# The start of a one-core layer stack and the order of its recurrence: x split in quarters, six banks for the first tiles, T before U, all masks made ahead

## The chip, the cores and the metric

One core of a Trainium2 chip runs the whole kernel. The metric is the device time of one execution in microseconds, as the median over runs. The engines are TensorE (PE), VectorE (DVE), ScalarE (ACT), GpSimd (POOL) and SyncE (SP), which here only issues transfers. Each has its own instruction stream, in order; they meet through semaphores.

## What is computed

The kernel computes three layers over 256 tokens of 2048 channels. The change touches the start of the first layer and its recurrence. In short form:

```python
h = rms_norm(x, norm_g)
proj = h @ w_in                       # all projections of the first layer
q, k, v, ... = split(proj)            # windowed attention, memory attention
mkv = rms_norm(mem, mem_norm_g) @ x_w_kv
# recurrence, per head, forward and backward in time (12 heads, two directions):
def step(S, inp):
    r_t, d_t, k_t, v_t, kk_t, b_t = inp
    sa = einsum('bhij,bhj->bhi', S, -kk_t)
    S = S * d_t[:, :, None, :] + sa[..., None] * b_t[:, :, None, :] + v_t[..., None] * k_t[:, :, None, :]
    return S, einsum('bhij,bhj->bhi', S, r_t)
```

The normalisation is folded in late: x is multiplied by its gain and goes into the products raw, and each result tile is scaled by one over the root mean square (rstd) when it leaves its bank.

## The kernel before

**Products.** Every weight matrix comes from memory as a stream of 565 tiles (128 output channels by 2048 inputs), each in two units of 8 blocks of 128 by 128, 512 KB. A ring of four units holds them: SP loads `raw`, ACT copies it to `w_hi` (`split_hi`, L284 to L294), DVE writes the rest to `w_lo` (`split_lo`, L296 to L303), and PE does three matmuls of 256 columns for each block (`product`, L310 to L316): high by high, high by low, low by high. The result of a tile gathers in bank 0 or 1 by the tile's parity. A unit's slot is split anew once PE has used it (`units_used`), and loaded anew once its `w_lo` is made (`lo_ready`). `hx` holds x times gain, split in the same way (`act_tile` L381, `dve_tile` L385), 16 blocks.

**Start.** SP issues the first four units. ACT issues `par`, the four quarters of x, the constants, the four quarters of mem and three small tensors (L2687 to L2695), then splits: unit 0, eight blocks of x, unit 1, eight blocks, two more units. DVE follows in the same order, with unit 0 ahead of the x blocks. PE's first tile needs eight blocks of x (`ready`). POOL squares and sums x block by block (L394 to L400), two operations each, then mem in the same way. After tile 1 PE multiplies the sum by ones into bank 2 (`x_norm.pe`, L413), ACT takes the root (L417), DVE the reciprocal (L421), and only then does the first of the 14 tiles of phase `plain` leave its bank (L451). Within the phase ACT's and DVE's streams hold the splitting of mem behind tiles 0 and 1, eight blocks each (L383, L388).

**Recurrence.** `act_rwkv`, `dve_rwkv`, `pool_rwkv` and `pe_rwkv` loop over six pairs of heads. Four weight tiles per pair (`pair_tile`, 64 blocks) run beside it on PE in portions set out by hand: `go(GO_START)` 8 blocks, `go(GO_PREP)` 24, three times `go(GO_GRAM)` 7, the rest one at a time. PE's first matmuls of a pair (`zw`) feed a tanh on ACT (L1055); a chain on DVE (L1102 to L1120) makes decays and keys; then PE forms the products within chunks (`mt`, `kat`, `m`, L1204). Tile 2 of a pair is split on DVE in `dve_pair_tile(v, p, 0)`, behind that chain. The inverse of a 64 by 64 triangle is built in five levels: PE makes X from the masked matrix `ml` and `tm`, ACT copies it (L1082), PE makes U and then T for one direction and then for the other, DVE adds them to `u` (L1160) and `tm` (L1157). POOL makes each level's `ml` (L1043) in one buffer a direction, after PE has used the last.

## Time and profile before

| | us |
|---|---|
| median of 3 runs (lowest, highest) | 3683.31 (3678.11, 3684.11) |
| the profiled execution | 3684.94 |
| its span | 3683.1 |
| PE busy | 3537.9 (96%) |
| DVE busy | 2404.0 (65%) |
| ACT busy | 1627.7 (44%) |
| POOL busy | 366.7 (10%) |

The span runs from the first to the last instruction of the profiled execution; 1.8 us lie around it. Busy PE is summed over its matmuls, whose ends are modelled, so a busy stretch can hide short gaps. The first PE instruction is at 21.25 us. The phase `plain` ends near 126.66 us, the recurrence lies between about 398 and 764 us, six pairs of 61.6 us.

### The profile page before, as it was taken

How to read it: one execution, taken by the hardware profiler on the slowest of the kernel's cores; microseconds unless marked ns; L12 is line 12 of the kernel's file. 1: busy time of each engine (PE TensorE's matmuls, PEld its weight loads, DVE VectorE, ACT ScalarE, POOL GpSimd, SP SyncE). 2: the span in 40 equal slices, each digit the busy share in tenths (PEclk: the TensorE clock that was granted, in tenths of full speed). 3: DMA queues.
4: the chain of work that ended last, by engine and by line, in shares of the span. 5: the costliest groups of instructions: out<-in, count | busy, mean ns of one | idle time of the engine just before them, and what ended most of it. 6: DMA issues, size and time to landing. Idle time of an engine off the chain costs nothing.

```text
span 3683.1 us, 76895 instructions
## 1 busy us (share of the span) xinstructions
PE 3537.9 (96%) x28942; PEld 3295.8 (89%) x28942; DVE 2404.0 (65%) x3377; ACT 1627.7 (44%) x2205; POOL 366.7 (10%) x417
## 2 busy tenths in 40 slices
PE   6999899999999999989999999999999799999997
PEld 6999888889999999989988888889999788888886
DVE  6787666665565467866666666676675665656567
ACT  4456333334444433654444444444344443434344
POOL 6000232310011000221100000010000300000004
PEclk9999999999999999999999999999999999999999
DMA  5544221225565555445565555555544455556564
GB/s 201 164 155 145 87 81 61 81 93 182 182 203 186 183 172 171 149 143 180 180 192 180 190 185 189 181 190 187 182 157 147 142 177 188 194 183 193 182 189 154
DMA packets 165417, 606.14 MB, mean 165 GB/s; under 512 B 18384, under 2 KB 18512, under 8 KB 164992
## 3 DMA queue, kind: packets, MB, share of 16 engines
q1 hardware_dynamic: 163296, 594.62, 50.2%
q10 hardware_dynamic: 1760, 6.80, 0.5%
q8 instruction: 136, 2.23, 0.3%
q0 software_dynamic: 192, 2.23, 0.2%
q14 instruction: 33, 0.27, 0.0%
HBM read 601.47 MB, written 2.10 MB: 164 GB/s over the span
## 4 chain that ended last, share of the span: by engine, by line
PE 86%; DVE 10%; ACT 2%; issue 2%; ACTq 0%; DVEq 0%; POOL 0%
PE bank L329 25%; PE bank L314 14%; PE bank L316 14%; PE bank L315 14%; PE bank L330 13%; PE bank L1204 4%; DVE w_lo L303 3%; ACT w_hi L294 0%; ACT X L2595 0%; DVE mem_hl L388 0%; DVE hx L388 0%; DVE xa L1782 0%; PE bank L1410 0%; DVE tm L1157 0%; DVE nrm_kk L925 0%
## 5 line engine op out<-in xcount | busy, mean ns | idle before, releaser
L294 ACT ACTIVATE w_hi<-raw 128x1024 fp32r<-128x1024 f32 x1130 | 1161.3, 1052 | 905.7 <-PE bank L316 537.8
L303 DVE TENSOR_TENSOR w_lo<-raw,w_hi 128x1024 fp32r<-128x1024 f32 x1130 | 1372.0, 1253 | 103.6 <-ACT w_hi L294 103.4
L329 PE MATMUL bank<-hid,w_hi 128*128 128x512 f32 x2048 | 717.5, 395 | 1.3 <-DVE hid L2025 1.2
L330 PE MATMUL bank<-hid,w_lo 128*128 128x256 f32 x2048 | 572.6, 280 | 0.0
L314 PE MATMUL bank<-hx,w_hi 128*128 128x256 f32 x1568 | 462.7, 295 | 42.4 <-DVE hx L388 23.9
L329 PEld LDWEIGHTS bank<-hid,w_hi 128*128 128x128 f32 x2048 | 384.0, 188 | 93.7 <-issue 2.2
L315 PE MATMUL bank<-hx,w_hi 128*128 128x256 f32 x1568 | 448.3, 286 | 0.0
L316 PE MATMUL bank<-hx,w_lo 128*128 128x256 f32 x1568 | 447.7, 286 | 0.0
L330 PEld LDWEIGHTS bank<-hid,w_lo 128*128 128x128 f32 x2048 | 386.4, 189 | 0.0
L329 PE MATMUL bank<-xh,w_hi 128*128 128x512 f32 x1024 | 358.5, 395 | 19.3 <-issue 17.7
L314 PE MATMUL bank<-u,w_hi 128*128 128x256 f32 (+1 forms) x1280 | 366.8, 287 | 9.5 <-DVE w_lo L303 9.5
L316 PE MATMUL bank<-u,w_lo 128*128 128x256 f32 (+1 forms) x1280 | 367.5, 287 | 0.0
L315 PE MATMUL bank<-u,w_hi 128*128 128x256 f32 (+1 forms) x1280 | 367.1, 287 | 0.0
L329 PE MATMUL bank<-u,w_hi 128*128 128x512 f32 x1024 | 360.6, 397 | 1.0 <-DVE w_lo L303 1.0
L314 PEld LDWEIGHTS bank<-hx,w_hi 128*128 128x128 f32 x1568 | 304.7, 194 | 55.3 <-DVE hx L388 24.2
L315 PEld LDWEIGHTS bank<-hx,w_hi 128*128 128x128 f32 x1568 | 305.1, 195 | 1.0 <-issue 1.0
L316 PEld LDWEIGHTS bank<-hx,w_lo 128*128 128x128 f32 x1568 | 305.1, 195 | 0.0
L330 PE MATMUL bank<-u,w_lo 128*128 128x256 f32 x1024 | 287.3, 281 | 0.0
L330 PE MATMUL bank<-xh,w_lo 128*128 128x256 f32 x1024 | 286.8, 280 | 0.0
L314 PEld LDWEIGHTS bank<-u,w_hi 128*128 128x128 f32 x1280 | 244.0, 191 | 10.9 <-DVE w_lo L303 10.7
L329 PEld LDWEIGHTS bank<-xh,w_hi 128*128 128x128 f32 x1024 | 192.6, 188 | 64.4 <-issue 18.1
L315 PEld LDWEIGHTS bank<-u,w_hi 128*128 128x128 f32 x1280 | 244.8, 191 | 0.0
(453 smaller groups left out, 6393.4 us busy)
## 6 DMA issues: line engine op xcount, KB each, us to landing
raw<-stream SPq DMA_DIRECT2D x1130, 512.0 KB, 4.1
x_raw<-xT ACTq DMA_DIRECT2D x4, 512.0 KB, 10.4
mem_raw<-memT ACTq DMA_DIRECT2D x4, 512.0 KB, 18.0
x_res<-xT POOLq DMA_DIRECT2D x1, 2048.0 KB, 8.4
out<-X SPq DMA_DIRECT2D x4, 512.0 KB, 2.6
cst<-consts ACTq DMA_DIRECT2D x1, 1504.0 KB, 15.0
w_sb<-w ACTq DMA_DIRECT2D x1, 384.0 KB, 19.5
a_sb<-a ACTq DMA_DIRECT2D x1, 384.0 KB, 19.9
```

The lines of the kernel that those rows point to most:

```text
L294: nc.scalar.activation(w_hi[:, slot], raw[:, slot], ACT.Copy).then_inc(hi_ready, 1)
L303: nc.vector.tensor_tensor(w_lo[:, slot], raw[:, slot], w_hi[:, slot].bitcast(F), ALU.subtract).then_inc(lo_ready, 1)
L314: nc.tensor.matmul(dst, w_hi[:, slot, j], hi, start=first, stop=False)
L315: nc.tensor.matmul(dst, w_hi[:, slot, j], lo, start=False, stop=False)
L316: return nc.tensor.matmul(dst, w_lo[:, slot, j], hi, start=False, stop=last)
L329: nc.tensor.matmul(bank[:], w_hi[:, slot, j], both, start=kt == 0, stop=False)
L330: last = nc.tensor.matmul(bank[:, T:], w_lo[:, slot, j], hi, start=False, stop=kt == KT - 1)
L1204: last = nc.tensor.matmul(out[h], lhs[h], rhs[h], start=start, stop=stop)
```

## The change

The four quarters of x and the constants move from ACT's queue to SP's, in the order x quarter 0, unit 0, the other quarters, units 1 to 3, constants. ACT issues only `par` at first, runs a one-element activation, and splits x a quarter at a time; DVE splits four blocks before unit 0's low part, the other twelve behind it. PE's first tile waits for x by quarters. ACT squares x after its splits, POOL sums the squares, and mem is issued after the squares, the small tensors later still. Phase `plain` is written out tile by tile: tiles 2 to 5 go to banks 4 to 7, weights are split four tiles ahead of the first scaling, and the statistic is taken after tile 3. Mem is split two blocks a tile from tile 4 on. In the recurrence PE makes T before U, five buffers a direction hold the masks and POOL makes them in a row, the first unit of tile 2 is split at the head of the pair's loop on ACT and DVE, and PE starts a pair's first tile when the last pair's tile 2 (not 3) has left its bank. The lists of step names follow.

```diff
+PLAIN_BANKS, PLAIN_AHEAD = 6, 4
 CENTRED = {7: (0, 1), 8: (2, 3), 9: (4, 5), 10: (6, 7), 11: (8, 9), 12: (10, 11), 13: (12, 13), 14: (14,)}
...
-            def pe(self, pe):
-                pe.wait_ge(self.sums, 2 * KT + 1)
+            def act_square(self, act, kt, squares, squared):
+                nc.scalar.activation(squares[:, kt], self.src[:, kt], ACT.Square).then_inc(squared, 1)
+            def pool_squares(self, pool, squares, squared):
+                self.pool_start(pool)
+                pool.wait_ge(self.lo, KT)
+                for kt in range(KT):
+                    pool.wait_ge(squared, kt + 1)
+                    pool.wait_ge(self.sums, kt + 1)
+                    nc.gpsimd.tensor_tensor(self.acc[:], self.acc[:], squares[:, kt], ALU.add).then_inc(self.sums, 1)
+            def pe(self, pe, count=2 * KT + 1):
+                pe.wait_ge(self.sums, count)
                 nc.tensor.matmul(banks[2][:, 0:self.n], const("ones"), self.acc[:], start=True, stop=True).then_inc(self.stat, 1)
...
+        x_squares = at("x_squares", Z, [P, KT, T])
+        x_squared = sem("x_squared")
+        warm, warm_set = at("warm", Z + 20 * K, [P, 1]), sem("warm_set")
         mem_out, plain_out = (sem(n) for n in ("mem_out", "plain_out"))
+        def plain_bank(t):
+            return banks[2 + t] if 2 <= t < PLAIN_BANKS else banks[t % 2]
+        def dve_plain(v, late):
+            for t in range(COUNT["plain"]):
+                tile = Tile(FIRST["plain"], t)
+                if t == 0:
+                    for k in range(PLAIN_AHEAD):
+                        split_lo(v, Tile(FIRST["plain"], k).later())
+                    x_norm.dve_rstd(v)
+                tile_done(v, tile)
+                nc.vector.tensor_tensor(pl[:, t], plain_bank(t)[:, 0:T], x_norm.rstd[:], ALU.mult).then_inc(plain_out, 1)
+                if t >= PLAIN_AHEAD:
+                    split_lo(v, tile.later())
+                hooked(tile, late)
+        def act_plain(act, hooks):
+            for t in range(COUNT["plain"]):
+                tile = Tile(FIRST["plain"], t)
+                if t == 0:
+                    for k in range(PLAIN_AHEAD):
+                        split_hi(act, Tile(FIRST["plain"], k).later())
+                if t >= PLAIN_AHEAD:
+                    split_hi(act, tile.later())
+                hooked(tile, hooks)
+        def pe_plain(pe, after):
+            for t in range(COUNT["plain"]):
+                tile = Tile(FIRST["plain"], t)
+                if t in (PLAIN_BANKS, PLAIN_BANKS + 1):
+                    pe.wait_ge(plain_out, t - PLAIN_BANKS + 1)
+                elif t >= PLAIN_BANKS + 2:
+                    pe.wait_ge(plain_out, t - 1)
+                for q in range(4):
+                    if t == 0:
+                        pe.wait_ge(x_norm.lo, 4 * q + 4)
+                    pe.wait_ge(lo_ready, tile.units(q // 2 + 1))
+                    for kt in range(4 * q, 4 * q + 4):
+                        last = product(plain_bank(t)[:, 0:T], hx, (2 * tile.parity + q // 2) % RING, kt % HALF, kt, kt == 0, kt == KT - 1)
+                    if q % 2 == 1:
+                        last.then_inc(units_used, 1)
+                hooked(tile, after)
...
-            for k, n in enumerate(("abd", "rbd", "bbd", "kbd", "mt", "tm", "brt", "btok", "ktok", "nkatv", "kat", "krt", "u", "x", "ml")):
+            for k, n in enumerate(("abd", "rbd", "bbd", "kbd", "mt", "tm", "brt", "btok", "ktok", "nkatv", "kat", "krt", "u", "x")):
                 w[n] = at(f"{n}{d}", o + K * k, [P, NCH, CH])
+            w["ml"] = {l: at(f"ml{l}_{d}", o + 13 * K + K * l, [P, NCH, CH]) for l in range(1, LEVELS)}
             for k, n in enumerate(("e1", "e2", "e3", "th")):
...
-                        + [f"{n}{l}_{d}" for d in D2 for n in (("U", "T") if l < LEVELS - 1 else ("U",))]]
+                        + [f"{n}{l}_{d}" for d in D2 for n in (("T", "U") if l < LEVELS - 1 else ("U",))]]
                      + [f"{n}{s}_{d}" for s in ST for n in ("W", "SA", "S", "Y") for d in D2
...
-                        pe.wait_ge(gate_kept, p * BESIDE + max(k // KT - 1, 0))
+                        if p > 0 or k >= 2 * KT:
+                            pe.wait_ge(gate_kept, p * BESIDE + k // KT - 1)
                     if kt % HALF == 0:
...
                         for d, w in enumerate(dirs):
-                            need(pool, rw_p, f"X{l - 1}_{d}", p)
-                            rw_o.done(nc.gpsimd.tensor_tensor(w["ml"][:], w["mt"][:], level(l), ALU.mult), f"ml{l}_{d}")
+                            if l == 2 and d == 0:
+                                need(pool, rw_v, "q", p)
+                            rw_o.done(nc.gpsimd.tensor_tensor(w["ml"][l][:], w["mt"][:], level(l), ALU.mult), f"ml{l}_{d}")
                 need(pool, rw_p, f"X{LEVELS - 1}_1", p)
...
             with act.Fori(0, PAIRS) as p:
+                split_hi(act, pair_tile(p, 0).later(), (0,))
...
                     rw_a.done(nc.scalar.activation(w["e3"][:], w["s"][:], ACT.Exp, scale=HALF_DECAY), f"e3{d}")
-                split_hi(act, pair_tile(p, 0).later())
+                split_hi(act, pair_tile(p, 0).later(), (1,))
                 split_hi(act, pair_tile(p, 1).later())
...
-                            need(act, rw_p, f"T{l - 1}_{d}", p)
+                            need(act, rw_p, f"U{l - 1}_{d}", p)
                         rw_a.done(nc.scalar.activation(w["x"][:], value_part(bank_of(d, 1), 0), ACT.Copy), f"X{l}_{d}")
...
             with v.Fori(0, PAIRS) as p:
+                split_lo(v, pair_tile(p, 0).later(), (0,))
...
                 rw_v.done(nc.vector.tensor_tensor(rkv[:, p], rkv[:, p], ks[:], ALU.mult), "q")
-                dve_pair_tile(v, p, 0)
+                dve_pair_gate(v, p, 0)
+                split_lo(v, pair_tile(p, 0).later(), (1,))
...
                             rw_v.done(nc.vector.tensor_tensor(w["tm"][:], w["tm"][:], value_part(bank_of(d, 0), 0), ALU.add), f"T{l}_{d}")
-                        else:
-                            need(v, rw_p, f"U{l}_{d}", p)
+                        need(v, rw_p, f"U{l}_{d}", p)
                         rw_v.done(nc.vector.tensor_tensor(w["u"][:], w["u"][:], value_part(bank_of(d, 2), 0), ALU.add), f"U{l}_{d}")
...
                             need(pe, rw_v, f"T{l - 1}_{d}", p)
-                        rw_p.done(each(bank_of(d, 1), w["ml"], w["tm"]), f"X{l}_{d}")
+                        rw_p.done(each(bank_of(d, 1), w["ml"][l], w["tm"]), f"X{l}_{d}")
...
                             need(pe, rw_v, f"U{l - 1}_{d}", p)
-                        rw_p.done(each(bank_of(d, 2), w["x"], w["u"]), f"U{l}_{d}")
                         if l < LEVELS - 1:
                             rw_p.done(each(bank_of(d, 0), w["u"], w["x"]), f"T{l}_{d}")
+                        rw_p.done(each(bank_of(d, 2), w["x"], w["u"]), f"U{l}_{d}")
                 for s in ST:
...
         def _(sp):
-            for k in range(RING):
+            def x_in(q):
+                sp.dma_start(x_raw[:, 4 * q:4 * q + 4], xT[:, 4 * q:4 * q + 4]).then_inc(in_x[q], 16)
+            def raw_first(k):
                 sp.dma_start(raw[:, k], stream[k]).then_inc(raw_in[k], 16)
+            x_in(0)
+            raw_first(0)
+            for q in range(1, 4):
+                x_in(q)
+            for k in range(1, RING):
+                raw_first(k)
+            sp.dma_start(cst[:], consts).then_inc(in_cst, 16)
             rounds = N_UNITS // RING
...
         def _(pool):
-            for norm, parts in ((x_norm, in_x), (mem_norm, in_mem)):
-                norm.pool_start(pool)
-                for q in range(4):
-                    pool.wait_ge(parts[q], 16)
-                    for j in range(4):
-                        norm.pool_tile(pool, 4 * q + j)
+            x_norm.pool_squares(pool, x_squares, x_squared)
+            mem_norm.pool_start(pool)
+            for q in range(4):
+                pool.wait_ge(in_mem[q], 16)
+                for j in range(4):
+                    mem_norm.pool_tile(pool, 4 * q + j)
             pool_rwkv(pool)
...
             act.dma_start(par[:], params).then_inc(in_par, 16)
-            for q in range(4):
-                act.dma_start(x_raw[:, 4 * q:4 * q + 4], xT[:, 4 * q:4 * q + 4]).then_inc(in_x[q], 16)
-            act.dma_start(cst[:], consts).then_inc(in_cst, 16)
+            act.wait_ge(warm_set, 1)
+            nc.scalar.activation(warm[:], warm[:], ACT.Identity)
+            act.wait_ge(in_par, 16)
+            def split_x(q):
+                act.wait_ge(in_x[q], 16)
+                for kt in range(4 * q, 4 * q + 4):
+                    x_norm.act_tile(act, kt)
+            split_x(0)
+            split_hi(act, Tile(0, 0), (0,))
+            for q in range(1, 4):
+                split_x(q)
+            split_hi(act, Tile(0, 0), (1,))
+            split_hi(act, Tile(0, 1))
+            for kt in range(KT):
+                x_norm.act_square(act, kt, x_squares, x_squared)
             for q in range(4):
                 act.dma_start(mem_raw[:, 4 * q:4 * q + 4], memT[:, 4 * q:4 * q + 4]).then_inc(in_mem[q], 16)
-            act.dma_start(w2_sb[:], w2).then_inc(in_lora, 16)
-            act.dma_start(a2_sb[:], a2).then_inc(in_lora, 16)
-            act.dma_start(wgu_sb[:], wgu).then_inc(in_lora, 16)
-            def split_all(norm, parts, half=(0, 1)):
-                for kt in range(HALF * half[0], HALF * (half[-1] + 1)):
-                    if kt % 4 == 0:
-                        act.wait_ge(parts[kt // 4], 16)
-                    norm.act_tile(act, kt)
-            split_hi(act, Tile(0, 0), (0,))
-            act.wait_ge(in_par, 16)
-            split_all(x_norm, in_x, (0,))
-            split_hi(act, Tile(0, 0), (1,))
-            split_all(x_norm, in_x, (1,))
-            split_hi(act, Tile(0, 1))
             def after_plain0():
                 x_norm.act_root(act)
                 act_lam(act)
-                split_all(mem_norm, in_mem, (0,))
-            act_split_phase(act, "plain", {0: after_plain0, 1: lambda: split_all(mem_norm, in_mem, (1,)), 8: lambda: act_squares(act, 0),
-                                           10: lambda: act_roots(act, range(4)), 12: lambda: act_squares(act, 1)}, peel=COUNT["plain"] // 2)
+                act.dma_start(w2_sb[:], w2).then_inc(in_lora, 16)
+                act.dma_start(a2_sb[:], a2).then_inc(in_lora, 16)
+                act.dma_start(wgu_sb[:], wgu).then_inc(in_lora, 16)
+            def split_mem(kt):
+                if kt % 4 == 0:
+                    act.wait_ge(in_mem[kt // 4], 16)
+                mem_norm.act_tile(act, kt)
+                mem_norm.act_tile(act, kt + 1)
+            def with_mem(t, f):
+                return (lambda: (split_mem(2 * (t - 4)), f())) if t in range(4, 12) else f
+            own = {8: lambda: act_squares(act, 0), 10: lambda: act_roots(act, range(4)), 12: lambda: act_squares(act, 1)}
+            act_plain(act, {0: after_plain0, **{t: with_mem(t, own.get(t, lambda: None)) for t in range(4, 13)}})
...
         def _(v):
-            def split_all(norm, half=(0, 1)):
-                for kt in range(HALF * half[0], HALF * (half[-1] + 1)):
-                    norm.dve_tile(v, kt, kt + 1)
+            nc.vector.memset(warm[:], 0.0).then_inc(warm_set, 1)
+            v.wait_ge(in_par, 16)
+            for kt in range(4):
+                x_norm.dve_tile(v, kt, kt + 1)
             split_lo(v, Tile(0, 0), (0,))
-            v.wait_ge(in_par, 16)
-            split_all(x_norm, (0,))
+            for kt in range(4, KT):
+                x_norm.dve_tile(v, kt, kt + 1)
             split_lo(v, Tile(0, 0), (1,))
-            split_all(x_norm, (1,))
             split_lo(v, Tile(0, 1))
-            dve_scaled_phase(v, "plain", x_norm, pl, plain_out, {0: lambda: x_norm.dve_rstd(v)},
-                             {0: lambda: split_all(mem_norm, (0,)), 1: lambda: split_all(mem_norm, (1,)),
-                              **{11 + b: lambda b=b: dve_factors(v, [b]) for b in range(3)}}, peel=COUNT["plain"] // 2)
+            def split_mem(kt):
+                for k in (kt, kt + 1):
+                    mem_norm.dve_tile(v, k, k + 1)
+            late = {t: lambda t=t: split_mem(2 * (t - 4)) for t in range(4, 11)}
+            late[11] = lambda: (split_mem(14), dve_factors(v, [0]))
+            late[12], late[13] = lambda: dve_factors(v, [1]), lambda: dve_factors(v, [2])
+            dve_plain(v, late)
             dve_scaled_phase(v, "mem_kv", mem_norm, mkv, mem_out, {0: lambda: mem_norm.dve_rstd(v)}, {0: lambda: dve_factors(v, [3]), 1: lambda: dve_factors(v, [4]), 2: lambda: dve_factors(v, [5]),
...
                 pe.wait_ge(in_cst, 16)
-                x_norm.pe(pe)
-            plain_phase(pe, "plain", hx, plain_out, before=lambda k: x_norm.ready(pe, k), after={1: x_stat, 9: lambda: pe_stats(pe, range(4)), 13: lambda: pe_stats(pe, (4, 5))}, peel=COUNT["plain"] // 2)
+                x_norm.pe(pe, KT + 1)
+            pe_plain(pe, {3: x_stat, 9: lambda: pe_stats(pe, range(4)), 13: lambda: pe_stats(pe, (4, 5))})
```

## Rows read from the trace of the kernel before

**Rows 1.** Windows: busy us (and count) by engine, clock, DMA share, GB/s.
```profile
0.00:21.25 21.25, 0.00 (x0) 0.00 (x0) 8.07 (x10) 10.44 (x20) 11.96 (x21) 1.00 0.92 354
21.25:71.20 49.95, 38.56 (x242) 37.55 (x243) 39.13 (x40) 19.98 (x32) 43.72 (x50) 0.86 0.44 148
71.20:126.66 55.46, 55.46 (x443) 53.55 (x442) 30.35 (x29) 25.09 (x25) 0.00 (x0) 1.00 0.54 173
```

**Rows 2.** Timeline, PE, first 70 us: start, length, instruction [idle before <-releaser].
```profile
21.25 0.58 PE L314 MATMUL bank<-hx,w_hi 128*128 128x256 f32 x1 [21.25 <-DVE hx L388]
...
44.39 0.55 PE L314 MATMUL bank<-hx,w_hi 128*128 128x256 f32 x1 [4.16 <-DVE w_lo L303]
```

**Rows 3.** Windows (columns as rows 1): PE before and after the clock rises.
```profile
44.40:47.70 3.30, 3.30 (x15) 3.30 (x16) 3.30 (x4) 3.30 (x7) 3.06 (x4) 0.50 0.62 179
47.70:51.70 4.00, 4.00 (x35) 3.96 (x33) 4.00 (x6) 3.83 (x9) 3.54 (x6) 0.99 0.31 119
```

**Rows 4.** DMA issues: KB each, median us from issue to landing.
```profile
par<-params ACTq DMA_DIRECT2D x1, 241.0 KB, 4.1
```

**Rows 5.** Timeline, ACT: the start of the kernel.
```profile
3.88 2.23 ACTq L2692 DMA_DIRECT2D mem_raw<-memT  x4
...
10.80 1.28 ACT L294 ACT_TABLE_LOAD   x1 [10.80 <-issue]
12.09 1.06 ACT L294 ACTIVATE w_hi<-raw 128x1024 fp32r<-128x1024 f32 x1
13.06 3.29 ACT L383 ACTIVATE hx<-x_raw,par 128x256 fp32r<-128x256 f32 x8
```

**Rows 6.** Timeline, ACT: two neighbouring 256-column operations in a head pair.
```profile
649.13 0.40 ACT L1065 ACTIVATE e<-sx 128x256 f32<-128x256 f32 x1
649.44 0.40 ACT L1066 ACTIVATE e<-s 128x256 f32<-128x256 f32 x1
```

**Rows 7.** Timeline, DVE: splits, with POOL at work (first two) and without.
```profile
14.65 6.54 DVE L388 SCALAR_TENSOR_TENSOR hx<-x_raw,par,hx 128x256 fp32r<-128x256 f32 x8
...
42.81 2.98 DVE L303 TENSOR_TENSOR w_lo<-raw,w_hi 128x1024 fp32r<-128x1024 f32 x2
...
71.75 2.35 DVE L303 TENSOR_TENSOR w_lo<-raw,w_hi 128x1024 fp32r<-128x1024 f32 x2
...
397.78 2.45 DVE L931 SCALAR_TENSOR_TENSOR kkn<-rkv,par,nrm_kk 128x256 f32<-128x256 f32 x6
```

**Rows 8.** Groups, first 70 us: busy us, mean ns | idle before.
```profile
L400 POOL TENSOR_TENSOR x_norm_acc<-x_norm_acc,x_norm_sq 128x256 f32<-128x256 f32 x16 | 13.8, 865 | 1.3
```

**Rows 9.** Timeline, PE: one head pair of the recurrence (636 to 664 us).
```profile
641.63 0.38 PE L314 MATMUL bank<-hx,w_hi 128*128 128x256 f32 x1 [0.63 <-DVE rkv L971]
...
656.08 0.68 PE L1204 MATMUL bank<-abd,bbd 64*64 64x64 f32 x16 [0.81 <-DVE e_end L1120]
...
660.00 0.36 PE L314 MATMUL bank<-hx,w_hi 128*128 128x256 f32 x1 [0.90 <-DVE w_lo L303]
```

**Rows 10.** Timeline, ACT and DVE: the start of the same pair.
```profile
645.49 1.28 ACT L1055 ACT_TABLE_LOAD   x1 [3.39 <-PE bank L1226]
646.78 0.47 ACT L1055 ACTIVATE th<-bank,hw_sb 128x256 f32<-128x256 f32 x1
...
647.29 0.29 DVE L1102 TENSOR_SCALAR th<-th 128x256 f32<-128x256 f32 x1 [3.44 <-ACT th L1055]
```

**Rows 11.** Timeline, PE: the same place of the first head pair.
```profile
411.07 0.68 PE L1204 MATMUL bank<-abd,bbd 64*64 64x64 f32 x16 [2.45 <-DVE e_end L1120]
```

**Rows 12.** Timeline, PE: first matmuls (X) of levels 1, 2, 4 and 5.
```profile
673.98 1.15 PE L1204 MATMUL bank<-tm,ml 64*64 64x64 f32 x32
...
677.06 1.13 PE L1204 MATMUL bank<-tm,ml 64*64 64x64 f32 x21
...
683.35 1.48 PE L1204 MATMUL bank<-tm,ml 64*64 64x64 f32 x32
...
686.50 1.48 PE L1204 MATMUL bank<-tm,ml 64*64 64x64 f32 x32
```

2 lines of the change are left out of this document (1 added, 1 removed).

## The prediction

> **What bounds the kernel now.** I read the windows first, cut at the places where PE's work changes, then PE's timeline at the start, then the streams of DVE and ACT, and last one head pair. Between 71.20 and 126.66 us PE has no idle time at all, and ahead of that it has plenty [rows 1]: nothing for 21.25 us, then 38.56 us of busy time in 49.95 us, at a mean clock of 0.86. So the end moves one for one with the moment at which PE's stream is unbroken. A tile's length at full speed is in the same row: nine tiles of 48 matmuls and some 3.5 us of statistics fill 55.46 us, which is 5.77 a tile, 0.12 a matmul; I use 5.76.
>
> Five tiles end by 71.20. Five times 5.76 and 0.45 for the statistic's matmul are 29.25 us; PE took 71.20. The other 41.95 us are 21.25 of start, 11.39 idle (49.95 less 38.56) [rows 1] and 9.3 of slow clock. The idle parts end on DVE: the start on a split of x, a later one of 4.16 us on `w_lo` [rows 2]. Behind most of these gaps PE runs at half clock, 1.2 GHz, for some 3.3 us (clock 0.50, 15 matmuls in 3.30 us) before it is back at 2.4 GHz (35 in 4.00) [rows 3]. DVE is the late one because it is slow and has too much in front. Eight blocks of x take it 6.54 us, 0.82 each, while POOL works; an operation of the same kind and shape without POOL takes 0.41 (six in 2.45). Two weight units take 2.98 with POOL and 2.35 without [rows 7]. And the first scaling waits for POOL's sum, a root and a reciprocal, with eight blocks of mem behind it.
>
> **The start, worked out.** ACT is now the longest chain. `par` is issued at 0.75 us and takes 4.1 us [rows 4]; it leads its queue before and after, so ACT starts at 4.85, its table load (1.28 us, now ending at 12.09) being done under that wait [rows 5]. Then: sixteen x blocks at 3.29 / 8 = 0.41, 6.6 us; four weight units at 1.0 (1.06 long, with some overlap), 4.0 us [rows 5]; sixteen squares. Before has no square of this shape; two neighbouring operations of it without a per-partition scale stand 0.31 apart [rows 6], with one 0.41 [rows 5], so 5.0 to 6.6 us, and I take 5.0, since a square has no such scale. Four issues of mem take 2.2 us [rows 5]. That puts ACT at 22.7; I add 0.3 for quarters of x that arrive just in time (`par`, unit 0 and four quarters are 2.9 MB, wanted at 10.9; at the 354 GB/s of the start [rows 1], with 2 us of silence taken off, 3.2 MB have come by then). First unit of tile 2: 1.06 on ACT and 1.2 on DVE (2.35 / 2) [rows 7], so 25.3 us.
>
> PE can begin tile 0 after four blocks of x and unit 0: ACT has these at 7.6, DVE's low part at 8.9. Its first two quarters run at half clock till 14.1. DVE, without POOL at 0.41 a block, is done with x at 12.9 right behind ACT, with unit 1 at 14.8, with tile 1's units at 16.2 and 17.4. So tile 0 ends near 17.8 and tile 1 near 23.5. PE then waits 1.8 us for tile 2. Gaps of that size are followed by the slow stretch in some places and not in others (the 2.45 us at 411.07 [rows 11] is followed by matmuls at full spacing, the 4.16 us is not [rows 2]); half of its 1.6 us, 0.8, goes into the sum. Tiles 2, 3, 4 and the statistic are 17.28 + 0.45. Tile 4 ends at 25.3 + 0.8 + 17.7 = 43.8 us; before it was 71.2. **Gain 27.4 us.**
>
> What hides the rest. POOL's sum: sixteen additions at 0.865 [rows 8] from 15.9, done at 29.8, wanted after tile 3 at 37.6. Root, reciprocal and four scalings end by 43, and tile 6, the first that needs a bank back, starts at 49.6; without the six banks it would be late. ACT has a root, two small operations with table loads and three issues before tile 6's split: free by 46, wanted 1 us of copy and 1.2 us of DVE ahead of 49.6. Per tile DVE then has a scaling (0.4), two units (2.4 to 3.0) and two mem blocks (1.6 with POOL), 5.0 of the 5.76 us. The last two mem blocks share tile 11 with a reciprocal, which makes DVE 1.3 us late there; PE needs that split four units later, so nothing.
>
> The bounds of this part: squares at 0.41 and no luck with the clock take 2.4 off; a first unit that lands and is split without any wait, with tile 2 following tile 1 at once, adds 2.6. So 25 to 30 for what rows price, and 21 if DVE's speed does not change (below).
>
> **The recurrence.** Three edits. (a) **T before U.** In a level PE does X, X, then four groups of 0.47 us. Level 1, whose second X waits for nothing, lasts 677.06 - 673.98 = 3.08 us; level 4 lasts 686.50 - 683.35 = 3.15, the second X waiting for DVE's late T [rows 12]. With T first that wait goes, and what is next is ACT's copy of X, which already sets level 1. So 0.07 for each of levels 2 to 5: 0.3 a pair, 1.7 us in six. (b) **The gate.** PE's start of a pair waits 0.63 us for tile 3's scaling [rows 9]; tile 2's was long ago: 0.6 in each of five pairs. (c) **Unit 0 of tile 2 early.** It removes 0.90 us of waiting for `w_lo` [rows 9] and puts something in front of the tanh. ACT's copy can only start when PE has used the slot, which is when PE starts `zw`; the table load goes with the first activation of the loop, so load and copy end 1.28 + 1.0 us after that, and DVE's 1.2 us split follows before the chain at L1102. Before, load and tanh took 645.49 to 647.25 [rows 10]. From PE's own start: DVE's chain begins 647.29 before; after, with PE 0.6 earlier, at 644.3 + 2.35 + 1.2 = 647.87. The idle time before `mt` grows from 0.81 [rows 9] to about 2.0, the 0.90 goes, and PE meets its next block at 659.5 where it was 660.00 [rows 9]. DVE's masks of `mt` come as much earlier, since one unit fewer lies ahead of them. So (b) and (c) together are 0.5 in each of five pairs, 2.5 us. The first pair has no gate to save and its ACT starts late, so there load, copy and split all lie on the chain: 1.76 later at 411.07 [rows 11], less 0.90, so 0.9 lost. Masks ahead: eight POOL operations of 0.7 to 0.9 follow the last of level 1's, in a stretch where DVE reads banks and not SBUF twice; no PE wait ends on POOL here before, so nothing gained or lost. **Gain 1.7 + 2.5 - 0.9 = 3.3 us**; between a loss of 0.5 (the chain pays 1.76 in every pair: 10.6 against 5.4, 3.0 and 1.7) and, by the third rival below, a gain of 10.
>
> **Sum.** 27.4 + 3.3 = 30.7 us. The profiled execution would be 3684.94 - 30.7 = 3654.2; it lies 1.6 above the median of the runs. Against the median: 3683.31 - 30.7 = 3652.6 us. About 0.2% (7 us) is what a measurement tells from no change.
>
> **Rivals.**
> DVE keeps 0.82 us a block (12%). That length is seen only with POOL at work [rows 7], and no row read here has this line without it. Then x is done at 19.9 instead of 12.9, unit 1 at 21.1, tile 2 starts near 31.4: gain 21 + 3, time 3659. For it: the line writes rounded values and takes a scale per partition, which L931 does only in part. Against it: the ratio of two to L931, with the same shape.
> The Trainium skill, page SBUF, State Buffer, section on who interferes with whom, says that a DVE operation with two SBUF inputs and a POOL operation that reads SBUF block each other for the whole instruction. By that rule the block falls to 0.41 once POOL is silent, which is the forecast; the trace has 0.82 and 0.41 in the two conditions but for different lines, so it agrees without proving it.
>
> The pair's head costs more than it saves (13%). If the load comes in front of the copy and a second one in front of the tanh, the chain has 1.28 us more in each of six pairs: 3.3 - 7.7 = 4.4 lost, time 3660. For it: six table loads now, one in each pair, so the loop forgets its set. Against: copies in the loop run after the tanh's set without a load.
>
> The table load is done before the slot's wait ends (12%). Then the chain begins 1.28 us earlier in each pair and PE's idle time at `mt` is back to 0.8: 7 us more, time 3646. For it nothing but order; the load at 645.49 waited for PE [rows 10].
>
> Slower than before (2%): POOL's sum is handed over square by square, and the scalings of all tiles hang on it. Tile 6 needs its bank at 49.6, and root, reciprocal and first scaling take 4 us. With 0.865 us a step the sum is there at 29.8 [rows 8]. From (45.6 - 15.9) / 16 = 1.9 us a step PE begins to stand, and from 1.9 + 30.7 / 16 = 3.8 us the kernel is slower than before. The slowest condition now, two operations a block under contention, is twice 0.865, 1.73. A time of 3690 needs 4.2.
>
> The change does little at the start because something unseen paces it, the arrival of x above all (3%): 3672.
>
> **Chances and range.** Forecast 58%, 3652.6. Range 3644 to 3662: it takes in the start between 21 and 30 and the recurrence between a loss of 4 (second rival) and a gain of 10, not all at their worst together. Faster by over 0.2%: 0.96; within 0.2%: 0.02; slower: 0.02.
>
> **What would show it.** First matmul near 9 us; DVE's x blocks 0.41 apart; tile 4's scaling at 44, phase `plain` over at 99 instead of 126.66. In a pair: no `w_lo` wait, no gate wait, about 2 us ending on `e_end`, levels of 3.08. What would make it wrong: x blocks at 0.82, a first matmul after 12, a second table load in a pair, or any wait in the later tiles of `plain` on rstd.

## The result and the profile after

The changed kernel takes 3645.99 us (median of 5 runs, 3641.99 to 3655.65) against 3684.11 of five runs of the kernel before taken beside it: 38.1 us less. The ratio estimated from the runs is 0.9888, 95% interval 0.9875 to 0.9902; the quotient of the two medians, 0.9897, lies inside that interval. Applied to the 3683.31 of the runs shown above, the ratio gives 3642, some 2 us under the lower end of the range (3644); the difference of 38.1 gives 3645, just inside it. The forecast was 3652.6, a gain of 30.7. The direction and the start were right; the recurrence gave some 11 us where I had 3.3. The third rival had 3646, nearer than the forecast.

The windows of after; the first two together cover the work of all three in [rows 1], the third the attention (columns as there: busy us and count by engine, clock, DMA share, GB/s):

```profile
0.00:44.20 44.20, 31.76 (x244) 31.39 (x245) 26.63 (x34) 29.38 (x52) 25.13 (x30) 1.00 0.90 342
44.20:99.40 55.20, 55.20 (x441) 53.28 (x440) 42.30 (x45) 31.24 (x41) 26.32 (x25) 1.00 0.53 166
99.40:370.00 270.60, 262.89 (x2077) 248.29 (x2075) 218.04 (x346) 146.10 (x215) 2.26 (x3) 1.00 0.48 150
```

Tile 4 is done at 44.2 instead of 71.2, nine tiles then take 55.2 without idle time as before, and `plain` ends at 99.4 instead of 126.66. The start, PE's idle times with what ended them:

```profile
9.93 0.55 PE L317 MATMUL bank<-hx,w_hi 128*128 128x256 f32 x1 [9.93 <-DVE w_lo L306]
...
15.82 0.36 PE L317 MATMUL bank<-hx,w_hi 128*128 128x256 f32 x1 [0.95 <-DVE w_lo L306]
```
```profile
37.75 0.67 PE L429 MATMUL bank<-x_norm_acc,cst 128*128 128x256 f32 x2 [1.55 <-POOL x_norm_acc L424]
```

and DVE in the same stretch:

```profile
6.50 1.67 DVE L391 SCALAR_TENSOR_TENSOR hx<-x_raw,par,hx 128x256 fp32r<-128x256 f32 x4 [5.62 <-ACT hx L386]
...
9.71 4.83 DVE L391 SCALAR_TENSOR_TENSOR hx<-x_raw,par,hx 128x256 fp32r<-128x256 f32 x12
...
44.21 0.42 DVE L476 TENSOR_TENSOR pl<-bank,x_norm_rstd 128x256 f32<-128x256 f32 x1 [1.93 <-PE bank L319]
```

The four blocks of x take 1.67 us and the next twelve 4.83, 0.40 each, against 6.54 for eight [rows 7]. The first matmul is at 9.93, one gap of 0.95 follows, and the only other one is new: 1.55 at 37.75 for POOL's sum, whose additions take 0.73 to 1.81 us each (ns least/median/most, then first and last start):

```profile
L424 POOL TENSOR_TENSOR x_norm_acc<-x_norm_acc,x_squares x16: 732/1132/1810, 16.7 to 36.1; 128x256 f32<-128x256 f32 x16
```

In the recurrence the waits of PE (line, who ended them: us, times, longest) were, in [rows 9], 0.63 for the gate, 0.81 on `e_end` and 0.90 for `w_lo`, in each pair. After:

```profile
PE bank L1274 <- DVE e_end L1190: 6.8, 6, 4.1
...
PE bank L1274 <- DVE u L1230: 0.4, 1, 0.4
```

The gate and `w_lo` are gone. `e_end` holds the first pair for 4.13 us and the other five for 0.53. ACT at the head of a pair shows why it isn't 2.0 as I had it:

```profile
606.82 1.06 ACT L297 ACTIVATE w_hi<-raw 128x1024 fp32r<-128x1024 f32 x1 [0.40 <-PE bank L319]
607.90 1.28 ACT L297 ACT_TABLE_LOAD   x1
609.70 1.06 ACT L297 ACTIVATE w_hi<-raw 128x1024 fp32r<-128x1024 f32 x1 [0.51 <-PE bank L319]
610.66 0.46 ACT L1124 ACTIVATE th<-bank,hw_sb 128x256 f32<-128x256 f32 x1
```

The first line is still the last pair's. The table load, 1.28 us, runs at 607.90, ahead of the wait for the slot that PE gives back, and is over 0.51 us before PE ends that wait at 609.70. The copy of unit 0 then starts at once and the tanh follows it.

**Where to measure.** The last phases scatter more than the change's parts are worth. From the first `ybd` (DVE, right behind the recurrence) to the end sixteen profiles, all with the same code there, take 2900.4 to 2917.4 us. A time of the whole kernel from one execution therefore says little about a change of 1 to 3 us. So single profiles are compared by three marks ahead of that: the last matmul on `pr` (end of the attention), PE's first matmul behind `e_end` in each pair, and the first `ybd`. Of before and after the first `ybd`:

```profile
L1377 DVE TENSOR_TENSOR ybd<-kkn,grs x2: 1751/1753/1755, 773.4 to 775.2; 64x1536 f32<-64x1536 f32 x2
```
```profile
L1447 DVE TENSOR_TENSOR ybd<-kkn,grs x2: 1751/1753/1755, 734.5 to 736.3; 64x1536 f32<-64x1536 f32 x2
```

773.4 and 734.5: 38.9 us, close to the 38.1 of the medians; the spans, 3683.1 and 3646.9, have 36.2, since after happened to be 2.7 slower behind the mark (2912.4 against 2909.7).

### The profile page after: what moved, and what is told of

It reads as the page before. It is cut to its first block, busy times and chain, and to the rows that moved or that the text cites. A ratio compares the mean times of both kernels' runs of the same rounds, so it can differ in the third digit from the quotient of the medians.

```text
span 3646.9 us, 76911 instructions
## 1 busy us (share of the span) xinstructions
PE 3532.4 (97%) x28942; PEld 3288.7 (90%) x28942; DVE 2394.9 (66%) x3378; ACT 1633.6 (45%) x2222; POOL 352.0 (10%) x401
## 3 DMA queue, kind: packets, MB, share of 16 engines
q10 hardware_dynamic: 1040, 3.16, 0.2%
## 4 chain that ended last, share of the span: by engine, by line
PE 86%; DVE 9%; ACT 3%; issue 2%; POOL 1%; DMA 0%; DVEq 0%; ACTq 0%; POOLq 0%
PE bank L332 26%; PE bank L317 14%; PE bank L318 13%; PE bank L319 13%; PE bank L333 13%; PE bank L1274 5%; DVE w_lo L306 2%; ACT w_hi L297 1%; POOL x_norm_acc L424 1%; DVE xa L1852 0%; ACT X L2665 0%; PE bank L1480 0%; DVE nrm_kk L990 0%; ACT x L1151 0%; DVE xa L1845 0%
```

## The experiments

All marks in us ("step" is the distance of two pairs' first matmul behind `e_end`, in the steady pairs; "recurrence" is last `pr` to first `ybd`, "rest" first `ybd` to the end of the span):

| kernel | last `pr` | first pair | step | first `ybd` | recurrence | rest |
|---|---|---|---|---|---|---|
| before | 387.0 | 411.07 | 60.99 | 773.4 | 386.4 | 2909.7 |
| after | 359.7 | 385.54 | 58.40 | 734.5 | 374.8 | 2912.4 |
| after_again | 359.9 | 387.15 | 58.40 | 736.1 | 376.2 | 2912.6 |
| start_only | 359.7 | 385.34 | 60.98 | 746.8 | 387.1 | 2902.2 |
| rec_only | 388.4 | 415.20 | 58.40 | 763.4 | 375.0 | 2906.2 |
| unit_late | 359.9 | 385.49 | 59.63 | 739.7 | 379.8 | 2914.8 |
| gate_back | 359.9 | 385.67 | 59.28 | 738.5 | 378.6 | 2914.0 |
| u_first | 359.8 | 385.60 | 58.90 | 737.0 | 377.2 | 2904.9 |
| masks_back | 359.8 | 385.59 | 58.40 | 734.3 | 374.5 | 2911.2 |
| late_load | 359.8 | 387.13 | 61.37 | 750.6 | 390.8 | 2913.6 |
| pool_squares | 367.2 | 393.04 | 58.40 | 742.0 | 374.8 | 2910.4 |
| two_banks | 375.0 | 400.79 | 58.40 | 749.0 | 374.0 | 2912.4 |
| x_on_act | 362.1 | 387.95 | 58.40 | 737.6 | 375.5 | 2912.0 |
| stat4 | 358.4 | 385.47 | 58.40 | 734.3 | 375.9 | 2900.4 |
| first_late | 359.7 | 383.54 | 58.40 | 731.4 | 371.7 | 2917.4 |
| both | 358.0 | 380.41 | 58.40 | 728.3 | 370.3 | 2911.6 |

A step of after's loop repeats within 0.02 us behind the first one, and the last `pr` of kernels with after's start within 0.2; rec_only, whose start is that of before, has it 1.4 later. The first step is longer by what the first pair's slow clock costs (59.95 in after). Seven profiles have some 5 us at a granted clock of 0.66 to 0.73 from the last `pr` on, which lengthens the column "recurrence" (by 1.4 in after_again against after): start_only, rec_only, after_again, unit_late, late_load, stat4 and first_late; the other nine have 1.00 there. Every row is one profile; unit_late, gate_back, u_first, masks_back, pool_squares, two_banks, x_on_act and first_late ran once and have no median.

**The two halves and the scatter.** start_only takes the transfers, quarters, squares on ACT and six banks; rec_only takes T ahead of U, unit 0, the gate and the masks; after_again is after itself.

> The start of after (order of transfers, quarters of x, squares of x on ACT, six banks) with the recurrence of before. By the two profiles the start is worth 27.2 us (scaling of tile 4 at 44.21 against 71.41), so the span should be 27 shorter than before and 9 longer than after, the median near 3656. If the missing part of the gain (the medians differ by 38.1, the two profiled executions by 36.2, my sum says 30.7) lay in the start, something behind tile 4 would be shorter too, and this kernel would gain 30 or more. In the recurrence a pair should be back at 61.56 us with 0.90 of waiting for w_lo and 0.6 for the gate.

> The start of before with the recurrence of after (T ahead of U, unit 0 of tile 2 ahead of the chain, no wait for tile 3's gate, masks ahead). Theory: the table load runs before the slot's wait ends, each pair is 2.48 us shorter (59.08), and the whole gain is 9 us, so a median near 3675 and a ratio near 0.9975. The forecast on record would have it at 3.3 us (3680, ratio 0.9991). If start and recurrence are independent, the gains of this kernel and of the start alone add up to that of after.

> After, unchanged, to see how much of 38.1 against 36.2 us is the scatter of runs. Theory: the profile's 36 us are the change's worth and the medians of few runs move by 2 to 4 us; the ratio then lies between 0.988 and 0.991, the span within 1 us of 3646.9. Rival: the change has a further effect of 4 us that one profile does not show; then the ratio is again 0.9888 or lower and the difference of the spans is 40.

Measured: start_only 3662.17 us (3650.78 to 3671.01, 5 runs), ratio 0.9940 (0.9925 to 0.9954); rec_only 3673.83 (11 runs), 0.9964 (0.9953 to 0.9976); after_again 3646.64 (4 runs), 0.9889 (0.9875 to 0.9904), beside 3686.37 of before. By the marks the first `ybd` comes 26.6 earlier with the start alone, 10.0 with the recurrence alone, 38.9 and 37.3 with both. The sum of the parts, 36.6, is 2.3 and 0.7 short of that; 1.4 of it is what rec_only is late at its last `pr`, ahead of anything that it changes. So start and recurrence are independent as far as this scatter lets one see. By the marks start_only is where it was expected (26.6 for 27), while its median is 6 us above the 3656 expected; the part behind the marks scatters by more than that. after_again's span, 3648.7, was expected within 1 us of 3646.9; rec_only was expected at 3675, with a gain of 9. The second profile of after has the 1.6 in one place, half clock for a few matmuls behind the attention's last wait. The same stretch in after, then in after_again (columns as rows 1, clock third from the end):

```profile
359.60:364.60 5.00, 5.00 (x44) 5.00 (x43) 2.39 (x3) 2.91 (x4) 0.00 (x0) 1.00 0.44 142
```
```profile
359.60:364.60 5.00, 5.00 (x31) 5.00 (x32) 2.51 (x3) 1.86 (x4) 0.00 (x0) 0.66 0.44 146
```

Like with like, the recurrence is 11.6 us shorter (before's 386.4 to after's 374.8, both at full clock there) or 10.9 (start_only's 387.1 to after_again's 376.2, both with that stretch).

**The parts of the recurrence, each undone alone.**

unit_late, in ACT's loop (in DVE's the same):

```diff
-                split_hi(act, pair_tile(p, 0).later(), (0,))
...
-                split_hi(act, pair_tile(p, 0).later(), (1,))
+                split_hi(act, pair_tile(p, 0).later())
```

gate_back, in PE's tiles beside the pairs:

```diff
-                        if p > 0 or k >= 2 * KT:
-                            pe.wait_ge(gate_kept, p * BESIDE + k // KT - 1)
+                        pe.wait_ge(gate_kept, p * BESIDE + max(k // KT - 1, 0))
```

u_first (PE's matmuls and the waits of ACT and DVE to match), and masks_back, where `ml` is one buffer for each direction:

```diff
-                        + [f"{n}{l}_{d}" for d in D2 for n in (("T", "U") if l < LEVELS - 1 else ("U",))]]
+                        + [f"{n}{l}_{d}" for d in D2 for n in (("U", "T") if l < LEVELS - 1 else ("U",))]]
```

```diff
+                            need(pool, rw_p, f"X{l - 1}_{d}", p)
+                            rw_o.done(nc.gpsimd.tensor_tensor(w["ml"][:], w["mt"][:], level(l), ALU.mult), f"ml{l}_{d}")
```

> After with unit 0 of tile 2 copied and split behind the chain again, as before. Theory: the load goes to the tanh and waits for PE again, w_lo's 0.90 us of waiting is back, and the idle time ahead of mt goes from 0.53 to 0.8: a pair of 60.3 us instead of 59.08, the five intervals 300.5. Rival: the unit's place is worth nothing as such and the gain is gate, T and masks; then a pair stays under 59.5.

> After with PE waiting for tile 3's gate at the start of a pair again. Theory: 0.6 us of waiting in each of five pairs, and the chain starts that much later: a pair of 59.7, the five intervals 297.6. Rival: the head's other waits move up, DVE scales tile 3 in time, and the wait costs 0 to 0.2.

> After with U ahead of T in each level, as before. Theory: levels 2 to 5 wait for DVE's late T again, 0.07 each, and a wait of 0.4 for u stands in each pair: 59.4 to 59.8 a pair instead of 59.08, the five intervals 296.1 to 298. The forecast had 0.3 a pair for it. Rival: with the masks made ahead T is in time either way, and a pair stays at 59.1.

> After with one mask buffer in each direction, so that POOL makes each level's mask behind the X of the level before. The forecast had the masks at nothing, since no PE wait ends on POOL in before. Theory: a pair within 0.2 us of 59.08. Rival: the masks carry the part of the 2.48 us a pair that w_lo (0.90), the gate (0.63), T (0.3) and the idle time ahead of mt (0.3) leave, 0.3 a pair; then 59.4.

Measured: steps of 59.63, 59.28, 58.90 and 58.40 against 58.40, so unit 0 is worth 1.23 us a pair, the gate 0.88, T ahead of U 0.50 and the masks nothing. The sum, 2.61, is the whole difference of before and after (60.99 - 58.40 = 2.59). The expectations start from a pair of 59.08. That is the distance from the first start of `abd` (383.6) to the last (679.0) over five, which takes in the 1.8 us between the two directions of one pair and the first pair's 1.55 of half clock; the steady step is 58.40, and their absolute figures are too high by that. What they wanted on top (1.2, 0.6, 0.3 to 0.7, 0) is what came, but for the gate, which gave 0.88. PE's waits in unit_late, then one pair's gate in gate_back:

```profile
PE bank L1271 <- DVE e_end L1188: 6.5, 6, 2.5
PE bank L317 <- DVE w_lo L306: 5.4, 6, 0.9
```
```profile
609.27 0.28 PE L319 MATMUL bank<-hx,w_lo 128*128 128x256 f32 x1
610.18 0.39 PE L317 MATMUL bank<-hx,w_hi 128*128 128x256 f32 x1 [0.62 <-DVE rkv L1036]
610.40 0.28 PE L318 MATMUL bank<-hx,w_hi 128*128 128x256 f32 x1
```

0.90 for `w_lo` is back, and `e_end` is at 0.81 instead of 0.53: 1.18 of the 1.23. In gate_back the wait of 0.62 is seen. The other 0.26 of its 0.88 lie at the two ends of the gap, as the rows show: a matmul of this stream is given as 0.28 long but the next one starts 0.12 behind it when nothing waits, so a break costs 0.16 more than the idle time says, and the first matmul behind it holds the next one for 0.22 instead of 0.12. Of T ahead of U I had 0.07 in each of four levels. The X groups of levels 2 and 3 in u_first (with the wait behind the last level) and in after:

```profile
642.68 1.46 PE L1275 MATMUL bank<-tm,ml 64*64 64x64 f32 x32
...
645.82 1.48 PE L1275 MATMUL bank<-tm,ml 64*64 64x64 f32 x32
...
655.37 0.33 PE L1275 MATMUL bank<-nkatv,u 64*64 64x64 f32 x4 [0.41 <-DVE u L1231]
```
```profile
640.74 1.10 PE L1274 MATMUL bank<-tm,ml 64*64 64x64 f32 x32
...
643.85 1.10 PE L1274 MATMUL bank<-tm,ml 64*64 64x64 f32 x32
```

Levels of 3.14, 3.15 and 3.16 against three of 3.11 are 0.12 a pair; 0.41 is the wait for `u` behind the last level, which stood in five of the six pairs before and now stands only in the last. I had not counted it. (Together 0.53, for a measured 0.50.)

**The place of the table load.** late_load adds the slot's wait once more, ahead of everything in the pair:

```diff
             with act.Fori(0, PAIRS) as p:
+                act.wait_ge(units_used, pair_tile(p, 0).later().units(1 - RING))
                 split_hi(act, pair_tile(p, 0).later(), (0,))
```

> After with one more wait of ACT at the head of each pair, for the slot's last use, placed ahead of the table load, so that the load runs behind that wait as my forecast had it. Theory (the load hides behind the slot's wait): load, copy and DVE's split come 1.28 us later, PE's idle time on e_end grows from 0.53 to about 1.8 us, a pair from 59.08 to 60.4, the five intervals between the first and the last mt from 294.6 to 301, and the mark behind the recurrence (first ybd) from 735 to 741 to 743. Rival (the place of the load doesn't matter and my 3.3 us were wrong elsewhere): a pair stays at 59.1.

Measured: 3666.05 us (3657.09 to 3667.34, 4 runs), ratio 0.9942 (0.9923 to 0.9961); a step of 61.37, 2.97 more than after and even 0.4 more than before. The recurrence takes 390.8, longer than that of before. ACT and PE in one pair:

```profile
617.20 1.06 ACT L297 ACTIVATE w_hi<-raw 128x1024 fp32r<-128x1024 f32 x1 [0.40 <-PE bank L319]
620.20 1.28 ACT L297 ACT_TABLE_LOAD   x1 [1.94 <-PE bank L319]
621.49 1.06 ACT L297 ACTIVATE w_hi<-raw 128x1024 fp32r<-128x1024 f32 x1
622.46 0.46 ACT L1125 ACTIVATE th<-bank,hw_sb 128x256 f32<-128x256 f32 x1
```
```profile
632.49 0.97 PE L1275 MATMUL bank<-abd,bbd 64*64 64x64 f32 x16 [1.95 <-DVE e_end L1191]
633.24 1.07 PE L1275 MATMUL bank<-abd,kbd 64*64 64x64 f32 x16
634.10 1.07 PE L1275 MATMUL bank<-bbd,abd 64*64 64x64 f32 x16
```

The load now stands behind the slot's wait, as I had it in the forecast, and `e_end` costs 1.95 (I had 2.0). What neither the forecast nor the expectation (60.4 a pair, first `ybd` at 741 to 743) had is what follows: the groups of 16 matmuls stand 0.75 and 0.86 apart, where before has 0.51 and 0.47 behind the wait of 2.45 in [rows 11]. Before's next two groups, then the clock of that stretch in late_load and of the same one in after:

```profile
411.58 0.63 PE L1204 MATMUL bank<-abd,kbd 64*64 64x64 f32 x16
412.05 0.63 PE L1204 MATMUL bank<-bbd,abd 64*64 64x64 f32 x16
```
```profile
632.40:636.40 4.00, 3.91 (x80) 3.91 (x82) 3.58 (x10) 0.00 (x0) 0.02 (x1) 0.57 0.00 0
```
```profile
620.60:624.60 4.00, 3.90 (x104) 3.83 (x105) 3.58 (x10) 0.66 (x1) 0.02 (x1) 1.00 0.01 4
```

0.57 is a mix of the two levels, 2.4 and 1.2 GHz. From the first to the last of the six groups late_load takes 3.93 us and after 2.38, 1.55 more; with 1.42 of idle time that is the 2.97. (The 1.42 is 0.14 more than the load's 1.28; that rest is open.) So the place of the load is worth 3 us in each pair, more than the 2.59 of all the edits together.

**The start, one piece undone at a time.**

The edits of pool_squares (POOL squares x again, and ACT doesn't), two_banks, x_on_act (SP issues the weight units alone) and stat4:

```diff
-            x_norm.pool_squares(pool, x_squares, x_squared)
+            for norm, parts in ((x_norm, in_x), (mem_norm, in_mem)):
+                norm.pool_start(pool)
...
+                        norm.pool_tile(pool, 4 * q + j)
```

```diff
-PLAIN_BANKS, PLAIN_AHEAD = 6, 4
+PLAIN_BANKS, PLAIN_AHEAD = 2, 2
-            pe_plain(pe, {3: x_stat, 9: lambda: pe_stats(pe, range(4)), 13: lambda: pe_stats(pe, (4, 5))})
+            pe_plain(pe, {1: x_stat, 9: lambda: pe_stats(pe, range(4)), 13: lambda: pe_stats(pe, (4, 5))})
```

```diff
+            for q in range(4):
+                act.dma_start(x_raw[:, 4 * q:4 * q + 4], xT[:, 4 * q:4 * q + 4]).then_inc(in_x[q], 16)
+            act.dma_start(cst[:], consts).then_inc(in_cst, 16)
```

```diff
-            pe_plain(pe, {3: x_stat, 9: lambda: pe_stats(pe, range(4)), 13: lambda: pe_stats(pe, (4, 5))})
+            pe_plain(pe, {4: x_stat, 9: lambda: pe_stats(pe, range(4)), 13: lambda: pe_stats(pe, (4, 5))})
```

> After with POOL squaring and summing x as it arrives, as before, and no squares on ACT. Tests the term that carried the start: DVE's sixteen x blocks at 0.40 us without POOL. Theory: they go back to 0.82 (6.5 us more in all), tile 1 and tile 2 wait for DVE, and tile 4's scaling comes 3 to 6 us later than 44.2, although ACT has 5 us less to do and POOL's sum is there earlier. Rival (the block's length was set by what the line computes): they stay at 0.40, and with ACT free earlier tile 4 ends sooner than 44.2.

> After with two banks for the first tiles instead of six and the matmul of x's sum behind tile 1. Theory: PE stands behind tile 1 until POOL's sum is there (37.6), then for root, reciprocal and scaling (some 4 us), so tile 2 starts near 42 instead of 24: 15 to 20 us later, and PE behind it runs at half clock for 3 us. Rival: POOL adds faster while PE and DVE stand (0.87 instead of 1.30 a step), which gives 7 us of it back: 8 to 13.

> After with the quarters of x and the constants issued on ACT's queue behind par and the weight units alone on SP's. The forecast had the order of transfers at no cost of its own (x just in time, 0.3 us). Theory: ACT issues five more transfers (0.55 each) ahead of its table load, all under the wait for par, so the start moves by less than 1 us; what decides is the arrival of x and unit 0, which now share the engines sooner: first matmul 9.5 to 11.5, tile 4's scaling 43.5 to 46. Rival: arrival paces the start, the later x quarters wait behind four weight units, and tile 4 comes 3 us or more later.

> After with the matmul of x's sum behind tile 4 instead of tile 3. Theory: the 1.55 us that PE waits for POOL's additions at 37.75 us go (the sum is there at 37.6, tile 4 ends at about 42), while root, reciprocal and first scalings come some 4 us later and still precede tile 6's need of a bank at 49: 1.5 us less than after. Rival: the later scalings make PE wait for a bank at tile 6, 0.5 to 3 us, and the kernel is no faster than after.

pool_squares has its last `pr` 7.5 us later than after, and tile 4's scaling as much; 3 to 6 were expected. DVE and PE:

```profile
6.64 3.30 DVE L391 SCALAR_TENSOR_TENSOR hx<-x_raw,par,hx 128x256 fp32r<-128x256 f32 x4 [5.76 <-ACT hx L386]
...
11.53 9.82 DVE L391 SCALAR_TENSOR_TENSOR hx<-x_raw,par,hx 128x256 fp32r<-128x256 f32 x12
```
```profile
11.75 0.55 PE L317 MATMUL bank<-hx,w_hi 128*128 128x256 f32 x1 [11.75 <-DVE w_lo L306]
...
14.91 0.58 PE L317 MATMUL bank<-hx,w_hi 128*128 128x256 f32 x1 [0.26 <-DVE hx L391]
...
23.04 0.55 PE L317 MATMUL bank<-hx,w_hi 128*128 128x256 f32 x1 [5.30 <-DVE w_lo L306]
```

The same line in the same kernel, 0.82 us a block with POOL at work and 0.40 without: the rival that DVE keeps 0.82 is out. The rule of the Trainium skill (page SBUF, State Buffer, who interferes with whom), which the forecast could only set beside two different lines, is now borne out on one line as to the contention. That each engine stands still for the whole of the other's operation is not: while DVE stands idle a POOL operation of this shape takes 0.61 or 0.73 us (`mem_norm_sq` and `mem_norm_acc` in after, at 43.08 and 43.78), so with DVE's 0.40 strictly in turn a block would take 1.0 to 1.1 us, and 0.82 was measured. In PE's stream tile 2 waits 5.30 for its split. two_banks undoes three things at once (the banks, the place of the statistic, and weights split four tiles ahead) and costs 15.3 at `pr`; PE's gaps:

```profile
35.32 1.19 PE L429 MATMUL bank<-x_norm_acc,cst 128*128 128x256 f32 x2 [10.48 <-POOL x_norm_acc L424]
39.23 0.58 PE L317 MATMUL bank<-hx,w_hi 128*128 128x256 f32 x1 [2.72 <-DVE pl L476]
```

POOL's sum came at 35.3 instead of 37.75, so the rival's faster additions (18.4 us for sixteen instead of 20.9) gave back 2.4 us and not 7; the theory's 15 to 20 holds. Six banks with the sum behind tile 3 are the largest piece of the start. x_on_act costs 2.4: its first x block on ACT waits for `x_raw` till 8.50 instead of for `par` till 5.88, and PE begins at 12.55. The five issues take ACT's queue 2.6 us, all under a wait; what counted is that x landed later when its transfers were issued beside the weights' and not ahead of them. Tile 4's scaling came at 46.64, between the theory's 46 and the rival's 3 us. stat4 takes the new 1.55 us away: last `pr` 1.3 earlier, 3642.06 us (4 runs), ratio 0.9886 (0.9870 to 0.9902). At the first `ybd` only 0.2 to 1.8 us are left of it, since this profile has the slow stretch behind `pr` (clock 0.68), and the medians can't tell it from after.

**The first pair.** first_late writes the first pair out ahead of the loop, on ACT and DVE, and leaves unit 0 behind the chain there; `both` adds the edit of stat4.

```diff
-            with act.Fori(0, PAIRS) as p:
-                split_hi(act, pair_tile(p, 0).later(), (0,))
+            def one(p, head=False):
+                if not head:
+                    split_hi(act, pair_tile(p, 0).later(), (0,))
...
-                split_hi(act, pair_tile(p, 0).later(), (1,))
+                split_hi(act, pair_tile(p, 0).later(), (0, 1) if head else (1,))
...
+            one(0, True)
+            with act.Fori(1, PAIRS) as p:
+                one(p)
```

> After with the first pair written out ahead of the loop on ACT and DVE, and in it unit 0 behind the chain as before; pairs 2 to 6 as in after. Theory: the first wait on e_end falls from 4.13 to 2.45 us and the half clock behind it goes, while 0.90 of waiting for w_lo comes back: from the last weight of the attention (start of the last pr matmul) to the first ybd 2.3 us less than the 374.8 to 376.2 of after, and later pairs stay at 58.40. Rival: the long wait comes from ACT's lateness after the attention, whatever stands first; then e_end stays near 4. A second rival: code written out costs its own fetches, and the pair gains nothing.

> The first pair as in first_late, and the matmul of x's sum behind tile 4 as in stat4. Theory: 2.3 + 1.5 us less than after, a mark (first ybd) of 731 to 732.5 where after has 734.5 and 736.1, and a median of 3641 to 3643 against 3646 of after. Rival: the scatter of the later phases (2900 to 2913 us behind that mark in the profiles so far) covers it, and the medians do not tell it from after.

In after the first pair pays 4.13 us and half clock behind it; in the kernel `both` it pays 0.72 and 0.59:

```profile
385.54 0.68 PE L1274 MATMUL bank<-abd,bbd 64*64 64x64 f32 x16 [4.13 <-DVE e_end L1190]
386.06 0.97 PE L1274 MATMUL bank<-abd,kbd 64*64 64x64 f32 x16
386.82 1.06 PE L1274 MATMUL bank<-bbd,abd 64*64 64x64 f32 x16
```
```profile
380.41 0.68 PE L1282 MATMUL bank<-abd,bbd 64*64 64x64 f32 x16 [0.72 <-DVE e_end L1195]
...
384.01 0.36 PE L317 MATMUL bank<-hx,w_hi 128*128 128x256 f32 x1 [0.59 <-DVE w_lo L306]
```

The recurrence is 371.7 us in first_late (with the slow stretch behind `pr`; 376.2 in after_again) and 370.3 in `both` (without; 374.8 in after): 4.5 less, twice what I expected, since the wait on `e_end` fell not to 2.45 but to 0.7. ACT in first_late shows the rest:

```profile
374.49 0.48 ACT L1125 ACTIVATE th<-bank,hw_sb 128x256 f32<-128x256 f32 x1 [6.13 <-DVE kkn L996]
...
376.35 1.28 ACT L1134 ACT_TABLE_LOAD   x1
377.65 0.42 ACT L1134 ACTIVATE e<-s 128x256 f32<-128x256 f32 x1
```

Written out, the first tanh needs no table load, and the load stands ahead of the exponentials, where ACT in after waits 0.94 us for DVE anyway (at 378.31). In after's first pair the load stands behind ACT's wait for DVE's `kkn` (at 373.28, with 6.36 idle ahead of it), so there load and copy both delay the tanh. The kernel `both` takes 3642.05 us (3633.55 to 3648.00, 5 runs), ratio 0.9872 (0.9856 to 0.9889). Its first `ybd` is at 728.3, earlier than the 731 to 732.5 expected; after has 734.5 and 736.1. It is the best kernel of the study by that mark; its interval overlaps that of after, as its rival said.

## Why the prediction missed

**The start: right.** 27.2 by tile 4's scaling (44.21 against 71.41), 27.3 at the last `pr`, 26.6 at the first `ybd` with the start alone; forecast 27.4. Its terms were less good than its sum. First matmul at 9.93 instead of 8.9, since `par` was waited for till 5.88, 1.0 longer (its transfer took 5.1, not 4.1). The issues of mem, 2.2 us in my sum, cost ACT nothing: their rows (17.56 to 18.89) lie beside squares 0.31 apart, and tile 2's first copy ran at 21.11 instead of 23.0. That removed the gap of 1.8 before tile 2 with its 0.8 of slow clock. POOL's sixteen additions took 1.30 each instead of 0.865, ended at 37.6 instead of 29.8, and PE waited 1.55. Two late terms and one early one cancelled, so that the sum came within 0.2 us is luck in part; squares at 0.31 and x blocks at 0.40 were as worked out.

**T ahead of U: right mechanism, too small.** 0.50 a pair instead of 0.3. The forecast's own term, DVE's late T, gave only 0.12; the other 0.41 is the wait for `u` that it had left out.

**The gate: right mechanism, a little small.** 0.88 a pair instead of 0.6: the idle time was read rightly, and the 0.26 at its two ends were left out.

**Unit 0 ahead of the chain: the step that failed.** I wrote that "ACT's copy can only start when PE has used the slot [...] the table load goes with the first activation of the loop, so load and copy end 1.28 + 1.0 us after that". The copy does wait; the load does not. It runs while ACT waits, the chain starts 1.28 us earlier, and with the gate (b) and (c) are 2.11 a pair and not 0.5. That is the third rival. It had 7 us for five pairs at 12%, for which I saw "nothing but order"; late_load is the direct test: it adds one wait, for something that the copy waits for anyway, and so moves the load behind it, and it measures 2.97 a pair. The rows tell the two cases apart by where the idle time stands: in [rows 10] and in late_load the load itself is what PE releases (1.94 in late_load) and the activation follows without a pause; in after the load has no idle time ahead of it and the activation has 0.51. A wait in front of the load holds both, a wait between them holds the activation alone. I had read [rows 10] as if it held for every place. The source doesn't tell which of the two it will be: before's tanh and after's copy both have their `wait_ge` on the line above the activation, yet the load ran behind the first and ahead of the second. What decides it, no run here shows.

**A second error hid in the same step**: I took 1.2 us more of idle time in each pair at its face value. late_load shows that it would have brought half clock and 1.55 us on top. Had the load stood where I put it, (b) and (c) would have lost 2.97 - 2.11 = 0.86 us a pair instead of gaining 0.5, and the recurrence would have been 3.7 longer than before (390.8 against 387.1 in start_only, both with the slow stretch behind `pr`). That is nearly the size of the second rival, 4.4 lost, by another mechanism. The one question of where the load stands decided between the two ends.

**The first pair**: forecast 0.9 lost; 1.68 more on `e_end` as worked out (1.76), less the 0.90, but 1.55 of half clock behind a wait of 4.13. [rows 11] had shown none behind 2.45.

The sum by sections: last `pr` to `e_end` of the first pair 1.8 lost, five steps 12.4 gained, the last pair 0.9: some 11.6. With 27.3 that is 38.9.

## What to carry over

Before pricing an engine's table load, find in a trace on which side of the wait it stands: with the idle time on the load's own row, or on the row of the activation behind it. In the second case the load cost nothing here, since the wait was longer than it, and the copy at the loop's head became a place for the load to hide. For a place that no trace shows yet, give both cases a chance and a price. Price idle time on PE twice, as idle and as what the clock does behind it: here 0.5 to 0.8 and 2.45 us were free of it, 1.95 and 4.13 were not, and 2.3 was either. And where late phases scatter by 17 us, compare single profiles at a mark right behind the change.
